# A two-layer block network on one core: the mLSTM recurrence with rows spread by transfers, a halved Fourier product, and the clamp of the exponent limited to the diagonal block

## The chip, the cores and the metric

The kernel runs on one core of a Trainium2 chip. The metric is the device time of one execution in microseconds (us); lower is better. Matrix products run on TensorE (PE; PEld is its weight load), elementwise work on VectorE (DVE), ScalarE (ACT) and GpSimd (POOL), and SyncE (SP) issues the transfers.

## The reference, cut to what matters

A sequence of 512 positions with 1024 channels goes through two layers of a first kind (feed-forward, a mixer of three branches, feed-forward, an embedding gate) and two of a second kind. All of the change lies in the mixer of the first kind, which runs twice. One projection makes the inputs of the three branches (attention, mLSTM, Fourier), 16 of its columns (m_if) are the gates of the mLSTM, and 64 (k_rope) the rotary key:

```python
u = rmsnorm(h, mix_norm[i]) @ w_in[i]
c_q, c_kv, k_rope, m_x, m_v, m_o, m_if, f_in = split_cols(u, IN_SPLITS)
```

The mLSTM, for 4 heads in 2 directions, weights scores by an exponential of gate sums; b is the running sum of log forget gates, and only s <= t counts:

```python
D = jnp.where(causal, b[..., :, None] - b[..., None, :] + ic[..., None, :], -jnp.inf)
m_t = jnp.maximum(m_inter, jnp.max(D, axis=-1))
w_intra = jnp.exp(D - m_t[..., None])
s = jnp.einsum('bhtd,bhsd->bhts', qc, kc) * w_intra
h = numer / jnp.maximum(jnp.abs(denom), jnp.exp(-m_t))[..., None]
```

The Fourier branch takes the real part of a two-dimensional transform over 512 positions and 64 channels of a group, and maps it linearly:

```python
y = jnp.fft.fftn(zg, axes=(1, 3), norm='ortho').real.astype(z.dtype)
return jnp.einsum('bsgc,gce->bsge', y, w).reshape(B, S, FNET_WIDTH) + b
```

## The kernel before, in words

Everything is held transposed, channels on the 128 partitions and the 512 positions along a row. Weights stream through one ring for the whole program: SP loads a tile of 128x1024 numbers (`Ring.load`, L400) into one of three raw buffers, ACT rounds it to a high part (L412), DVE makes the low part (L422), and PE multiplies high by high, high by low and low by high (L334 to L336), so one 128x1024 tile against 1024x512 inputs is 8x3 products. The ring is four tiles deep.

The program is a list of stages. Each is a block in which every engine runs its own list and which ends in a barrier (L243): the next stage starts when all engines, SP with its waits among them, have come to the end. Three stages matter here, each run once per layer.

**Projection** (`Project1`, last part of a longer stage). 11 column tiles, of which number 9 holds the rotary key twice over and number 10 the 16 gate columns, padded to 128 (`in1_g`); then four row parts of the ring for v and the Fourier input. PE: `Project.pe`; DVE copies each tile out of PSUM with the norm's factor; ACT adds the gates' biases (L1537, L1538), SP then loads the maps of the attention (L1503, L1504).

**Attention** (`mixer1_attention`). DVE computes the gate rows of the mLSTM at its start: 8 rows (4 heads, 2 directions) of 512 numbers each, on partitions 0 to 3 and 32 to 35, in `rows_a`, `rows_m`, `rows_t` (L1769 to L1774, semaphore `rows_ready`); the last come when ACT has taken an exponent (L1717).

**Recurrence** (`mixer1_mlstm`). No chunks: each head and direction is one masked product over all 512 positions. 8 groups g (head pair p, direction d, half e), each of 4 steps j, one per block of 128 source positions; a step spans 512, 384, 256 or 128 target positions (`span`). The 32 steps go through five engines, in an order written out by hand:

- PE spreads the row of the group over 128 partitions with a product into bank 2 or 3 (`spread`, L1887), once per group, and the bound rows into bank 7 once per pair of groups (L1920);
- DVE adds a column and clamps at 0, over the whole span (L2015), into one of four buffers `wgt`;
- ACT takes the exponent of the span (L1968);
- DVE multiplies by the scores (L2024), POOL masks the diagonal block (L2052);
- PE multiplies by v (L1937; the last group's steps L1934), and the buffer is free (`used`).

DVE's list for iteration s is: argument of step s, weighting of step s-1, then, in iterations 2 to 6 of the eight of a pair of groups from the second pair on, the bound of the pair before (L1994, L1996) and four reciprocals (L2000). Between its steps PE also makes the scores (`scores`, L1875, 16 of them; ACT copies them out, L1880) and the Fourier branch in bank 4 (`fourier`: L1854 four sums of four products, L1856 two sums of two, L1858 two products; ACT copies out, L1865, L1867). At the end DVE finishes the last pair in pieces (L2035 to L2043) while PE runs 8 products whose result nobody reads (`idle_products`, L358).

```python
dve.wait_ge(m_spread, g + 1)
dve.wait_ge(used, s_ - 3)
V.tensor_scalar(wgt[:, s_ % 4, r], ps[2 + g % 2][:, r], acol[:, j, rc:rc + 1], 0.0, ALU.add, ALU.min)
```

## Time and profile before

| | |
|---|---|
| median of 3 runs | 3802.32 us (3802.03 to 3806.3) |
| profiled execution | 3797.43 us |
| its span in the trace | 3795.7 us |
| PE busy | 97% of the span, 16570 products and as many weight loads |
| DVE, ACT, POOL busy | 58%, 34%, 20% |
| mean granted TensorE clock | 0.972 of full speed |

The profiled execution is 4.9 us below the median, and its span 1.7 us below its own time. A product of full 32-bit numbers stands in the trace as two records. A record's duration is from its start to its modelled end, and successive records overlap, so the pace of PE is read from the starts.

### The profile page before, as it was taken

The numbers are of one execution on the slowest core, as the hardware profiler recorded it, in microseconds if no ns is written. First come the engines' busy times: TensorE is split into PE (matmuls) and PEld (weight loads), VectorE is DVE, ScalarE is ACT, GpSimd is POOL, SyncE is SP. The second block draws the span as 40 slices with busy tenths as digits, with TensorE's granted clock in tenths as the row PEclk, the third lists the DMA queues.
The fourth block names the chain that finished last, engine by engine and source line by source line (L and its number), as shares of the span: only waits on it lengthen the run. The fifth ranks groups of instructions, "written<-read, shape, count | busy, mean of one in ns | idle before, by whom it ended". The sixth has DMA issues, their size and how long they took to land. (4 is left out here: it accounts for less than half of the span.)

```text
span 3795.7 us, 41460 instructions
## 1 busy us (share of the span) xinstructions
PE 3683.5 (97%) x16570; PEld 2860.5 (75%) x16570; DVE 2212.1 (58%) x2936; ACT 1297.3 (34%) x1876; POOL 744.9 (20%) x448
## 2 busy tenths in 40 slices
PE   8999999999999999999999999999999999999999
PEld 6888744888878888546888876786888767867887
DVE  7655557655575555457755576565544556645444
ACT  3223235422242223334422344444222343543221
POOL 3432002244204330001434013120000020300000
PEclk9999999999999999999999999898999998989999
DMA  5443200444334443102444322002333220012332
GB/s 175 144 137 116 94 24 23 135 137 131 125 100 134 136 134 102 60 24 89 140 132 138 102 79 61 6 1 67 95 95 100 83 79 21 1 51 85 99 100 83
DMA packets 93087, 345.40 MB, mean 91 GB/s; under 512 B 10977, under 2 KB 11233, under 8 KB 92001
## 3 DMA queue, kind: packets, MB, share of 16 engines
q1 hardware_dynamic: 92896, 342.76, 28.2%
q8 instruction: 132, 2.16, 0.2%
q14 instruction: 59, 0.48, 0.0%
HBM read 340.62 MB, written 2.10 MB: 90 GB/s over the span
## 5 line engine op out<-in xcount | busy, mean ns | idle before, releaser
L412 ACT ACTIVATE w_hi<-raw 128x1024 fp32r<-128x1024 f32 (+2 forms) x540 | 558.5, 1037 | 1814.1 <-PE ps L336 1733.1
L334 PE MATMUL ps<-xs_hi,w_hi 128*128 128x512 f32 x2312 | 911.3, 394 | 2.5 <-DVE arena L1300 2.5
L336 PE MATMUL ps<-xs_hi,w_lo 128*128 128x512 f32 x2312 | 903.6, 391 | 0.0
L335 PE MATMUL ps<-xs_lo,w_hi 128*128 128x512 f32 x2312 | 903.4, 391 | 0.0
L422 DVE TENSOR_TENSOR w_lo<-raw,w_hi 128x1024 fp32r<-128x1024 f32 (+2 forms) x540 | 676.0, 1253 | 148.0 <-ACT w_hi L412 147.4
L334 PEld LDWEIGHTS ps<-xs_hi,w_hi 128*128 128x128 f32 x2312 | 436.3, 189 | 105.0 <-issue 14.9
L335 PEld LDWEIGHTS ps<-xs_lo,w_hi 128*128 128x128 f32 x2312 | 436.2, 189 | 93.8 <-issue 3.6
L336 PEld LDWEIGHTS ps<-xs_hi,w_lo 128*128 128x128 f32 x2312 | 436.2, 189 | 91.5
L334 PE MATMUL ps<-hd_hi,w_hi 128*128 128x512 f32 x1288 | 503.3, 391 | 1.5 <-DVE hd_lo L1037 1.5
L336 PE MATMUL ps<-hd_hi,w_lo 128*128 128x512 f32 x1288 | 501.2, 389 | 0.0
L335 PE MATMUL ps<-hd_lo,w_hi 128*128 128x512 f32 x1288 | 501.1, 389 | 0.0
L827 POOL TENSOR_SCALAR arena<-arena,parg 128x768 f32<-128x768 f32 x128 | 305.4, 2397 | 955.7 <-DMA arena<-in_ada 697.6
L1033 DVE TENSOR_TENSOR arena<-arena,ps 128x512 f32<-128x512 f32 x132 | 90.7, 687 | 355.4 <-PE ps L336 350.7
L334 PEld LDWEIGHTS ps<-hd_hi,w_hi 128*128 128x128 f32 x1288 | 241.7, 188 | 53.1 <-DVE hd_lo L1037 2.0
L335 PEld LDWEIGHTS ps<-hd_lo,w_hi 128*128 128x128 f32 x1288 | 241.8, 188 | 51.0 <-issue 1.0
L336 PEld LDWEIGHTS ps<-hd_hi,w_lo 128*128 128x128 f32 x1288 | 241.7, 188 | 50.2
L835 POOL TENSOR_TENSOR arena<-arena 128x768 f32<-128x768 f32 x112 | 224.5, 2004 | 9.6 <-POOL arena L833 0.6
L1028 DVE TENSOR_TENSOR arena<-ps,stream_rstd 128x512 f32<-128x512 f32 x132 | 91.2, 691 | 230.9 <-PE ps L336 230.5
L1059 DVE SCALAR_TENSOR_TENSOR arena<-ps,stream_rstd 128x512 f32<-128x512 f32 x96 | 66.4, 691 | 156.9 <-PE ps L336 156.1
L2190 POOL TENSOR_SCALAR arena<-arena,par 128x512 f32<-128x512 f32 x4 | 10.3, 2582 | 671.7 <-DVE arena L2392 671.3
L1062 DVE TENSOR_TENSOR stream<-stream,arena 128x512 f32<-128x512 f32 x144 | 112.3, 780 | 4.9
L334 PE MATMUL ps<-ys_hi,w_hi 128*128 128x512 f32 x256 | 101.4, 396 | 2.7 <-DVE w_lo L422 2.7
(480 smaller groups left out, 4624.0 us busy)
## 6 DMA issues: line engine op xcount, KB each, us to landing
raw<-in_ffn_gu SPq DMA_DIRECT2D x264, 512.0 KB, 3.8
arena<-in_ada SPq DMA_DIRECT2D x64, 768.0 KB, 5.7
raw<-in_ffn_dn SPq DMA_DIRECT2D x96, 448.0 KB, 3.3
raw<-in_in_t SPq DMA_DIRECT2D x60, 512.0 KB, 3.7
raw<-in_ffn_dn SPq DMA_DIRECT2D x48, 512.0 KB, 3.5
raw<-in_out SPq DMA_DIRECT2D x32, 512.0 KB, 3.8
raw<-in_pleg SPq DMA_DIRECT2D x16, 512.0 KB, 3.7
raw<-in_in_r SPq DMA_DIRECT2D x8, 512.0 KB, 3.9
```

The costliest lines, as they stand in the source:

```text
L334: T.matmul(bank, lhs_hi(k), rhs_hi(k), start=(first and k == 0), stop=False)
L335: T.matmul(bank, lhs_hi(k), rhs_lo(k), start=False, stop=False)
L336: mm = T.matmul(bank, lhs_lo(k), rhs_hi(k), start=False, stop=(last and k == kt - 1))
L412: A.activation(self.hi[:, n % HL, 0:size], raw[:, n % RAW, 0:size], ACT.Copy).then_inc(self.high_done, 1)
L422: V.tensor_tensor(self.lo[:, n % HL, 0:size], raw[:, n % RAW, 0:size], self.hi[:, n % HL, 0:size].bitcast(F32), ALU.subtract).then_inc(sel ...
L827: G.tensor_scalar(aw[:, e, :], aw[:, e, :], cond(k0 + e), None, ALU.mult).then_inc(self.scaled, 1)
L835: ins = G.tensor_tensor(a, a, aw[:, e, :], ALU.add)
L1028: V.tensor_tensor(gn[:, j % 2, :], ps[2 * (j % 2)][:, :], R[:, :], ALU.mult).then_inc(self.gate_read, 1)
L1033: V.tensor_tensor(hf[:, j % 2, :], gn[:, j % 2, :], ps[2 * (j % 2) + 1][:, :], ALU.mult).then_inc(self.up_read, 1)
L1059: V.scalar_tensor_tensor(out=tmp[:, o % 2, :], in0=ps[4 + o % 2][:, :], scalar=self.scales[o], in1=R[:, :], op0=ALU.mult, op1=ALU.mult).th ...
L1062: V.tensor_tensor(h[:, o, :], h[:, o, :], tmp[:, o % 2, :], ALU.add).then_inc(self.h_updated, 1)
L2190: G.tensor_scalar(cv[:, c, :], cx[:, c, 0:S], w_(0), None, ALU.mult).then_inc(self.tap, 1)
```

## The change

- **Gates.** The 16 gate columns move into the tile of the rotary key (64 + 16 + 48 of zeros); `in1_g` is gone, and the projection has 10 column tiles and one item less in the ring. ACT makes the key's second copy. The gates come out on partitions 64 to 79; SP moves them with four small transfers to the partitions where the bias step reads them, after `spread` and behind the two map loads in its list, and ACT waits for them (`gates_moved`).
- **Rows by transfers.** The two `spread` kinds of product are gone. SP sends each of the eight rows of `rows_m` to all 128 partitions with a transfer (each 128 x 2 KB = 256 KB written, read from a row on one partition) during the attention: five after `rows_ready` has come to 3, three after `copied` has come to 14; SP waits for all of them before that stage's barrier. The bound rows `rows_t` go the same way in the recurrence stage, eight transfers of 128 KB, behind the loads of the Fourier table; DVE waits for all eight before its first bound.
- **Clamp.** DVE adds and clamps only the diagonal block of 128 positions, now from SBUF; ACT takes the rest of the span's exponent straight from the spread row with the column as bias, as a second instruction in 24 of 32 steps.
- **Fourier.** The table holds 257 cosines and 255 sines side by side (1 MB instead of 2 MB), so the first sum gives half of the frequencies of both kinds in one bank: 8 products instead of 16; the second step has 8 products of half width instead of 4; the copy mirrors the rest. They are spread over the 32 steps, one each 7/4 steps, in banks 4 and 7.

The core of the diff:

```diff
-            columns(t["in1_g"][l, :, :], 1)
...
-            super().__init__(st, x, source, 11, S)
+            super().__init__(st, x, source, 10, S)
...
+            sp.wait_ge(self.spread, 1)
+            for g in range(2):
+                for d in range(2):
+                    r = HD + 2 * H * g + H * d
+                    sp.dma_start(gate_rows[g][32 * d:32 * d + H, :], kr_tmp[r:r + H, :]).then_inc(self.gates_moved, 16)
             sp.wait_ge(self.next_landed, 32)
...
             act.wait_ge(self.spread, 1)
+            for half in (slice(0, HD), slice(HD, P)):
+                A.activation(kr[half, :], kr_tmp[0:HD, :], ACT.Copy)
+            act.wait_ge(self.gates_moved, 64)
...
+                sp.wait_ge(rows_ready, 3)
+                for g, dst in enumerate((soft, lf, F, a, M)):
+                    r = mlstm_row(g)
+                    sp.dma_start(dst, rows_m[r:r + 1, :].unsqueeze(1).to_broadcast([1, P, S])).then_inc(m_spread, 16)
+                sp.wait_ge(copied, 14)
+                for g in range(5, 8):
+                    r = mlstm_row(g)
+                    sp.dma_start(m_rows[:, g - 5, :], rows_m[r:r + 1, :].unsqueeze(1).to_broadcast([1, P, S])).then_inc(m_spread, 16)
+                sp.wait_ge(m_spread, 128)
...
+        FOURIER_AT = [7 * f // 4 for f in range(18)]
+        COPIED_AT = [FOURIER_AT[f] + 1 for f in (3, 7, 11, 15, 16, 17)]
...
-                sp.dma_start(dft.rearrange("p a j s -> p (a j s)"), t["dft"]).then_inc(dft_landed, 16)
+                sp.dma_start(dft.rearrange("p j s -> p (j s)"), t["dft"]).then_inc(dft_landed, 16)
                 sp.dma_start(fw.rearrange("p a m -> p (a m)"), t["fnw"][l, :, :]).then_inc(dft_landed, 16)
...
+                for q in range(4):
+                    for e in range(2):
+                        r = mlstm_row(2 * q + e)
+                        sp.dma_start(thr[HD * e:HD * e + HD, q, :], rows_t[r:r + 1, :].unsqueeze(1).to_broadcast([1, HD, S])).then_inc(t_spread, 16)
...
-                for g in range(2):
-                    spread(pe, g)
...
-                        if 1 <= g < 7:
-                            spread(pe, g + 1)
...
-                            T.matmul(ps[7][:, :], pick_pair(36, 5 * d + p), rows_t[0:36, :], start=True, stop=True).then_inc(t_spread, 1)
+                    if s_ in FOURIER_AT:
+                        fourier(pe, FOURIER_AT.index(s_))
...
-                    A.activation(wgt[:, s_ % 4, span(g, j)], wgt[:, s_ % 4, span(g, j)], ACT.Exp).then_inc(exp_ready, 1)
+                    own, rest = slice(j * P, (j + 1) * P), others(g, j)
+                    ins = A.activation(wgt[:, s_ % 4, own], wgt[:, s_ % 4, own], ACT.Exp)
+                    if rest.start < rest.stop:
+                        rc = mlstm_row(g)
+                        ins = A.activation(wgt[:, s_ % 4, rest], m_of[g][:, rest], ACT.Exp, bias=acol[:, j, rc:rc + 1])
+                    ins.then_inc(exp_ready, 1)
...
-                dve.wait_ge(thr_ready, q + 1)
-                order.done(V.scalar_tensor_tensor(out=larger, in0=dens[q % 2], scalar=-1.0, in1=thr[:, q % 2, :],
+                dve.wait_ge(t_spread, 128)
+                order.done(V.scalar_tensor_tensor(out=larger, in0=dens[q % 2], scalar=-1.0, in1=thr[:, q, :],
...
-                        r = span(g, j)
-                        if s_ % ST == 0:
-                            dve.wait_ge(m_spread, g + 1)
+                        r = slice(j * P, (j + 1) * P)
...
-                        V.tensor_scalar(wgt[:, s_ % 4, r], ps[2 + g % 2][:, r], acol[:, j, rc:rc + 1], 0.0, ALU.add, ALU.min) \
+                        V.tensor_scalar(wgt[:, s_ % 4, r], m_of[g][:, r], acol[:, j, rc:rc + 1], 0.0, ALU.add, ALU.min) \
```

`mlstm_row(g)` gives the partition of group g's row: 0, 1, 32, 33, 2, 3, 34, 35.

## Rows read from the trace of the kernel before

**Rows 1.** The page, part 1: busy time and share of PE.

```profile
PE 3683.5 (97%) x16570; PEld 2860.5 (75%) x16570; DVE 2212.1 (58%) x2936; ACT 1297.3 (34%) x1876; POOL 744.9 (20%) x448
```

**Rows 2.** Windows of layer one: stretch, length, five engines' busy time, granted clock, DMA.

```profile
427.00:445.00 18.00, 18.00 (x79) 14.53 (x78) 9.48 (x8) 4.97 (x6) 0.00 (x0) 1.00 0.30 88
...
568.00:574.00 6.00, 5.80 (x10) 2.16 (x8) 1.91 (x4) 3.10 (x6) 0.92 (x2) 0.50 0.18 71
...
590.00:595.00 5.00, 5.00 (x13) 1.96 (x12) 3.49 (x8) 3.10 (x7) 1.18 (x3) 1.00 0.00 0
...
625.00:630.00 5.00, 5.00 (x8) 1.96 (x8) 4.96 (x10) 1.52 (x3) 1.08 (x3) 0.56 0.00 0
```

**Rows 3.** Timeline of PE, end of the projection: start, duration, line, operation.

```profile
442.75 0.39 PE L334 MATMUL ps<-xs_hi,w_hi 128*128 128x512 f32 x1
...
443.20 0.39 PE L336 MATMUL ps<-xs_hi,w_lo 128*128 128x512 f32 x1
```

**Rows 4.** Timelines of ACT and PE after the column tiles.

```profile
449.47 0.72 ACT L1538 ACTIVATE arena<-arena,par 4x512 f32<-4x512 f32 x1
466.12 1.57 ACT L1470 ACTIVATE arena<-ps,rowsum 128x256 f32<-128x256 f32 x4 [15.93 <-PE ps L336]
```

**Rows 5.** Timeline of PE in the recurrence of layer one.

```profile
561.95 1.52 PE L1887 MATMUL ps<-arena,consts 36*128 36x512 f32 x3 [0.94 <-PEq L243]
...
581.82 1.02 PE L1854 MATMUL ps<-arena 128*128 128x512 f32 x2
582.68 1.02 PE L1937 MATMUL ps<-arena 128*128 128x512 f32 x2
...
589.59 0.49 PE L1937 MATMUL ps<-arena 128*128 128x128 f32 x2
...
633.43 3.70 PE L1934 MATMUL ps<-arena 128*128 128x128 f32 x20
```

**Rows 6.** Waits from 562 to 637 us: who waited, total, times, longest.

```profile
DVE arena L2024 <- ACT arena L1968: 20.4, 11, 5.3
...
PEld ps L1854 <- DMA arena<-in_fnw: 1.5, 1, 1.5
```

**Rows 7.** Groups of instructions from 562 to 645 us: busy, mean ns, idle before.

```profile
L2024 DVE TENSOR_TENSOR arena<-arena 128x512 f32<-128x512 f32 (+3 forms) x32 | 17.5, 547 | 20.4 <-ACT arena L1968 20.4
...
L2015 DVE TENSOR_SCALAR arena<-ps,arena 128x512 f32<-128x512 f32 (+3 forms) x32 | 16.4, 514 | 11.8 <-PE ps L1887 11.7
L1968 ACT ACTIVATE arena<-arena 128x512 f32<-128x512 f32 (+3 forms) x32 | 14.8, 466 | 10.5 <-DVE arena L2015 10.4
L2052 POOL TENSOR_TENSOR arena<-arena,consts 128x128 f32<-128x128 f32 x32 | 14.7, 462 | 107.9 <-DVE arena L2024 107.9
...
L2000 DVE RECIPROCAL arena<-arena 128x128 f32<-128x128 f32 x12 | 11.3, 945 | 0.0
...
L1994 DVE SCALAR_TENSOR_TENSOR arena<-arena 128x512 f32<-128x512 f32 x3 | 2.3, 760 | 2.3 <-ACT arena L1949 2.3
```

**Rows 8.** Groups by shape: clamps and exponents of 128 columns, a DVE scaling from SBUF.

```profile
L2015 DVE TENSOR_SCALAR arena<-ps,arena 128x128 f32<-128x128 f32 x8 | 2.5, 312 | 0.1
...
L1968 ACT ACTIVATE arena<-arena 128x128 f32<-128x128 f32 x8 | 2.5, 306 | 5.9 <-DVE arena L2015 5.9
...
L1790 DVE TENSOR_SCALAR arena<-arena 128x1 f32<-128x1 f32 x16 | 2.5, 154 | 0.5
```

**Rows 9.** DVE's last gate row, then SP's first issue of the recurrence stage.

```profile
495.41 0.42 DVE L1774 COPY arena<-arena 4x512 f32<-4x512 f32 x1
...
562.00 0.33 SPq L1840 DMA_DIRECT2D arena<-in_dft  x1
```

**Rows 10.** DMA: a load of 256 KB, two tables; positions (one row to 128 partitions).

```profile
arena<-in_dft SPq DMA_DIRECT2D x2, 2048.0 KB, 7.4
...
arena<-in_ukv SPq DMA_DIRECT2D x2, 1024.0 KB, 8.8
...
positions<-in_pos SPq DMA_DIRECT2D x2, 256.0 KB, 9.0
...
arena<-in_mqk SPq DMA_DIRECT2D x2, 256.0 KB, 3.3
```

**Rows 11.** DMA from 9 to 17 us, when all 16 engines are busy.

```profile
DMA packets 1573, 3.18 MB, mean 398 GB/s; under 512 B 544, under 2 KB 544, under 8 KB 1573
```

**Rows 12.** Timeline of DVE: a weighting beside POOL's 128x512 products.

```profile
620.32 1.82 DVE L2024 TENSOR_TENSOR arena<-arena 128x512 f32<-128x512 f32 x1
```

More of the change, by code:

```diff
@@ L1549, in dve @@
                     V.memset(mx[:, :, S + 2:S + 4], 0.0)
+                    for rows_ in gate_rows:
+                        V.memset(rows_[0:32, :], 0.0)
                     for i in range(2):
@@ L1553, in dve @@
                 dve.wait_ge(ring.used, self.n0 + j + 1)
[L1554 removed]
+                V.tensor_tensor(dst[j], ps[j % 4][:, :], R[:, :], ALU.mult).then_inc(self.spread if j == 9 else self.copied, 1)
                 if j:
@@ L1593, in program @@
     kr_tmp = arena[:, SPARE_AT:SPARE_AT + S]
+    gate_rows = [arena[:, SPARE_AT + (1 + g) * S:SPARE_AT + (2 + g) * S] for g in range(2)]
     def rotate(dve, order, x, turned, table, tmp):
@@ L1809, in mixer1_mlstm @@
         wgt = sp_.get(4, S)
-        thr, larger = conv, absf
+        larger = absf
+        m_of = [soft, lf, F, a, M] + [m_rows[:, i, :] for i in range(3)]
         dens, nums = [sp_.get(S), second[:, 0, :]], [sp_.get(S), second[:, 1, :]]
@@ L1827, in span, with others @@
             return slice(j * P, S) if groups[g][1] == 0 else slice(0, (j + 1) * P)
+        def others(g, j):
+            return slice((j + 1) * P, S) if groups[g][1] == 0 else slice(0, j * P)
         with Stage() as st:
@@ new lines, in fourier @@
+            def fourier(pe, f):
+                if f < 8:
+                    j, k = divmod(f, 4)
+                elif f < 16:
+                    j, k = 2 + (f - 8) // 4, f % 4
+                else:
+                    j, k = f - 12, 0
+                c = j % 2
+                bank = ps[4 if j % 2 else 7]
+                if f == 0:
+                    pe.wait_ge(dft_landed, 32)
+                if j >= 2 and k == 0:
+                    pe.wait_ge(dft_copied, j - 1)
+                if j < 2:
+                    mm = T.matmul(bank[:, :], vz[:, k, 384 + c * P:384 + (c + 1) * P], dft[:, k, :], start=(k == 0), stop=(k == 3))
+                elif j < 4:
+                    src = part[:, c, MID + 1:S] if k % 2 else part[:, c, 1:MID] if k else part[:, c, 0:MID + 1]
+                    dst = bank[:, MID + 1:S] if k >= 2 else bank[:, 1:MID] if k else bank[:, 0:MID + 1]
+                    lhs = C("dft_c") if k % 2 == 0 else C("dft_n") if k == 3 else C("dft_s")
+                    mm = T.matmul(dst, lhs, src, start=(k % 2 == 0), stop=(k % 2 == 1))
+                else:
+                    mm = T.matmul(bank[:, :], fw[:, c, :], spec[:, c, :], start=True, stop=True)
+                if f in (3, 7, 11, 15, 16, 17):
@@ L1863, in fourier_copy @@
                 act.wait_ge(dft_done, j + 1)
-                if j < 6:
-                    ins = A.activation(part[:, j // 2, j % 2, :] if j < 4 else spec[:, j - 4, :], ps[4][:, :], ACT.Copy)
+                bank, c = ps[4 if j % 2 else 7], j % 2
+                if j < 2:
+                    ins = A.activation(part[:, c, :], bank[:, :], ACT.Copy)
+                elif j < 4:
+                    A.activation(spec[:, c, 0:MID + 1], bank[:, 0:MID + 1], ACT.Copy)
+                    ins = A.activation(spec[:, c, MID + 1:S], bank[:, S - 1:MID:-1], ACT.Copy)
                 else:
-                    ins = A.activation(y[:, j, :], ps[4][:, :], ACT.Identity, bias=col(l, c1, "fnet_b", j - 6))
+                    ins = A.activation(y[:, 6 + c, :], bank[:, :], ACT.Identity, bias=col(l, c1, "fnet_b", c))
                 ins.then_inc(dft_copied, 1)
@@ L1880, in scores_copy @@
                 A.activation(qks[:, m // 8, m % 2, m // 2 % ST, :], ps[m % 2][:, :], ACT.Copy).then_inc(qk_copied, 1)
-            def spread(pe, g):
-                p, d, e = groups[g]
-                if g >= 2:
-                    pe.wait_ge(arg_ready, ST * (g - 1))
-                T.matmul(ps[2 + g % 2][:, :], pick(36, 32 * d + 2 * p + e), rows_m[0:36, :], start=True, stop=True) \
-                 .then_inc(m_spread, 1)
             @st.block.tensor
             def _(pe):
-                for g in range(2):
-                    spread(pe, g)
                 for m in range(4):
@@ L1973, in _ @@
                         scores_copy(act, 6 + 2 * g + k)
-                    if k == 0 and e == 1:
-                        act.wait_ge(t_spread, q + 1)
-                        if q >= 2:
-                            act.wait_ge(dir_ready, q - 1)
-                        A.activation(thr[:, q % 2, :], ps[7][:, :], ACT.Copy).then_inc(thr_ready, 1)
                     if k == 1 and e == 0 and q:
@@ L3315, in lay_out @@
     cq, ckv, kr, mx, mv, mo, mif, fin = [w[:, :, o[i]:o[i + 1]] for i in range(8)]
-    f["in1_t"] = tile_pairs(np.concatenate([cq, ckv, mx, mo, kr, kr], 2))
-    gates = np.zeros((L, D, P), np.float32)
-    for g in range(2):
-        for d in range(2):
-            r = 64 * g + 32 * d
-            gates[:, :, r:r + H] = mif[:, :, 8 * g + 4 * d:8 * g + 4 * d + 4]
-    f["in1_g"] = rows(gates)
+    rest = np.zeros((L, D, 48), np.float32)
+    f["in1_t"] = tile_pairs(np.concatenate([cq, ckv, mx, mo, kr, mif, rest], 2))
     f["in1_r"] = rows(np.concatenate([mv, fin], 2))
```

91 lines of the change are left out of this document (34 added, 57 removed).

## The prediction

> **What bounds the kernel now.** The page comes first: PE is busy for 97% of the span, every other engine for 58% or less [rows 1]. So time comes off where PE has less to do, as long as PE is what the others wait for there. The windows say where that holds. In the projection PE is busy throughout at full clock and DVE half the time (427 to 445 us) [rows 2]. In the recurrence (562 to 637 us in layer one; layer two has the same shape) PE is busy too, but its clock is at the lower of its two levels (0.50, 1.2 GHz) after the barrier, back at the upper one by the middle, and low again from about 625 us [rows 2]. The waits and groups give the rest: POOL idles 107.9 us of DVE's weightings, DVE idles 11.7 us on the spread products and 20.4 us on ACT's exponents [rows 6, 7], which are late because ACT's list holds score copies that wait for PE. This stage is bound by PE first, and the DVE-ACT-DVE-POOL-PE round of a step stands right behind.
>
> **Part 1, the projection.** Starts of products lie (443.20 - 442.75)/2 = 0.225 us apart [rows 3]. One tile less is 24 products, 5.4 us per layer, and nothing covers it: the load, rounding and subtraction of a tile are all shorter than that. The detour of the gates is costed at nothing. Today the bias steps end at 450.2 us and ACT then has nothing until PE's row parts end at 466.1 [rows 4]. The four small transfers stand behind SP's two map loads, 8.8 us to landing for the later [rows 10]; ACT's two key copies and four bias steps (0.72 us each) follow. With everything 5.4 us earlier, the maps are issued near 443.5, the gates land near 454, the bias steps end near 457, and ACT is wanted at 460.7. Some 3.5 us of cover is left; beyond that, each us late is one lost at the next barrier.
>
> **Part 2, PE in the recurrence.** A full product of 512 columns takes 582.68 - 581.82 = 0.86 us at the upper clock [rows 5]. Gone are 8 spreads, 4 bound spreads, and of the Fourier branch's 22 products the worth of 8 (8 + 8 halves + 2 = 14): 20 x 0.86 = 17.2 us per layer. The last product now ends at 633.43 + 3.70 = 637.1 [rows 5], 75 us after SP's first issue of the stage [rows 9].
>
> I take the stage in its four pairs of groups. The first ends at 590.1, 28.1 us in [rows 5]. Off it go two spreads at low clock ahead of everything (1.9 us, from the 1.52 us for three of their four records), the wait for the Fourier tables (1.5 us [rows 6], the big one half as large) and, later, two spreads or bound spreads and three Fourier products (8 become 5), 5 x 0.86 = 4.3 us. That leaves 20.4 us.
>
> **Part 3, DVE, the next bound.** For each of the other pairs DVE has 8 weightings at 0.55, 8 clamps, a bound of two instructions at 0.76 and four reciprocals at 0.945 [rows 7]. A clamp of 128 columns from SBUF is not in the trace: 0.154 us (one column) and 0.312 us (128 columns from PSUM) are its ends [rows 8]; I take 0.2, since the fixed part dominates. Sum 4.4 + 1.6 + 1.5 + 3.8 = 11.3 us. Overlap of neighbours takes about 1 off, and meeting POOL puts something on. That meeting is in the trace: a weighting of 512 columns took 1.82 us beside POOL's large products [rows 12] against a mean of 0.55. I take 12.3 us a pair, between 10.3 (no meeting) and 15 (each of POOL's 0.46 us masks stops DVE once: 8 x 0.46 = 3.7 more). PE needs 4.3 us of products a pair, plus 1.7 to 5.5 of scores and Fourier, and fits.
>
> The Trainium skill has a rule that speaks against this part: "SBUF — State Buffer", section "Who interferes with whom", lets a single-source DVE instruction between SBUF operands take both ports and stop GpSimd for its whole length, which a clamp that reads PSUM does not. By it each clamp holds up a mask by its own 0.2 us or waits one out; the end of 15 us would be nearer. The weightings already show such stops; for clamps no row does.
>
> ACT's 24 extra instructions cost a fixed 0.2 us each (a 128-column exponent takes 0.306 [rows 8], for some 0.1 of columns), 1.2 us a pair; four threshold copies leave. ACT is busy for half the stage, so this is costed at nothing, and its price in a step's round, 0.2 us, is within the 12.3.
>
> Sum: 20.4 + 3 x 12.3 = 57.3, and 2.7 for the way through POOL and PE at the end and a low clock there: 60 us against 75, 15 per layer. The tail of DVE and the barrier stay as they are.
>
> **Part 4, the transfers.** This is the unknown. Eight of 256 KB may start when the last gate row stands, at 495.8 us, and the barrier falls just before 562.0 [rows 9]: 66 us of cover, which moves with everything else, so they are hidden up to 8 us each. The eight of 128 KB stand behind the Fourier table (3.7 us, half of 7.4 [rows 10]), while DVE's first bound comes about 23.5 us into the stage (20.4 and two steps): hidden if 0.8 + 3.7 + 4T < 23.5, where T is the time of 256 KB, so up to T = 4.7. The trace has no transfer out of SBUF of this kind. The low end is 256 KB in 3.3 us from issue to landing, alone [rows 10], of which the moving takes only 0.66 us at 398 GB/s [rows 11]. The high end by kind is the only broadcast of one row to 128 partitions, 9.0 us [rows 10], but that one stood in the crowd of the first loads, as the 398 GB/s around it show, and may have waited most of it. If one row's readers share a sixteenth of that rate, 25 GB/s, T is 10.5. I take the side of 3.3, being nearest in size and undisturbed: hidden.
>
> **The sum.** 2 x (5.4 + 15) = 41 us off. Against the profiled 3797.4 that is 3756.4; the median stands 4.9 us higher, so 3761 us.
>
> **Rivals.**
>
> A, slower: the source row is the limit. All eight rows lie on one partition each, and 16 engines read the same one. Place: SP's wait ahead of the attention's barrier, and DVE's wait at the first bound. Price per layer: the barrier comes 8T + 2 - 66 us later; the first bound comes at 4T + 4.5, and 1.5 for the bound and 22 steps at 1.54 (12.3/8) follow, so the last product ends at 4T + 40 against 75. With 5.4 gained, the net is 12T - 104.4: it turns at T = 8.7. At T = 9.6, between 9.0 and 10.5, the net is 10.8 us a layer, 3824 us in all. For it: the 9.0 us row, and that one partition cannot be expected to feed what 128 do. Against it: nothing in this trace is seen to be limited by its source. The Trainium skill gives a rule for it in "SBUF — State Buffer", section "Door 1: The DMA port swizzle": the rate depends on how many of 16 ports the partitions reach, partitions 0 to 3 and 32 to 35 share a single port, and four partitions were measured at 27.6 GB/s. By that rule T would be 9.5 us and the kernel slower; no run here shows it yet. Chance 0.34.
>
> B, half hidden: T between 4.7 and 8. The attention covers its eight, the bounds come late; at T = 6 the last product ends at 64, 11 us a layer from that stage, 3769 us. Chance 0.10.
>
> C, the meeting of DVE and POOL or the low clock: 15 us a pair. PE, with gaps between its bursts, may fall to its lower level, as it did after the gap before 625 us [rows 2], and then needs twice 6 to 10 us a pair. The stage loses 8 us of its gain, 3777 us. Chance 0.06.
>
> D, the change does not do what it says for the recurrence: the round of a step, not PE's amount, sets the pace, and the stage stays at 75 us. Only the projection is left, 3791 us. Against it stand windows with PE busy for all 5 of 5 us at full clock and DVE for 3.5 (590 to 595 us) [rows 2]. Chance 0.06.
>
> **How the numbers follow.** The forecast's own case has 0.44 and a range of its own, 3747 (10.3 us a pair: 12 us less in two layers) to 3772. A reaches from 3805 (T near 8.8) to beyond 3840. From 3747 to 3828, some 2 in 10 is left out: the upper part of A and the lowest of the forecast. 0.2% is 7.6 us, about what a measurement of this kernel can tell from no change. Faster by more: 0.43 of the forecast, 0.09 of B, 0.05 of C, 0.03 of D, 0.60. Slower by more: 0.29 of A. The rest, 0.11, is within.
>
> **What would show it.** Right: the projection's last tile ends 5.4 us earlier; the eight transfers of 256 KB land before the attention's last product, and SP is not the last at the barrier; DVE never waits for `t_spread`; the last product comes about 60 us into the stage, and DVE's idle time there is small. Wrong: the barrier waits for a transfer (PE idle for 10 us or more between attention and recurrence, as in A); one long idle time of DVE at the first bound, 23 us in (A, B); weightings or clamps well above their lengths beside POOL, or clock 0.50 in the middle of the stage (C); ACT waiting for `gates_moved` until after PE's row parts (part 1).

## The result, and the profile after

The changed kernel takes 3828.09 us (3827.43 to 3830.23, four runs) beside 3802.18 us of the kernel before on the same chip: 1.0074 of its time, with a 95% interval of 1.0059 to 1.0089. It is slower by 0.7%. That is rival A; the forecast's own case (3761) did not come, and the median lies 0.09 us above the range's upper end of 3828.

The table splits the executions of both kernels, and of two experiments told below, by stage. Projection is from SP's first load of `in_in_t` to its issue of `in_mqk`, attention from there to its issue of `in_dft`, recurrence from there to the first product of the ring behind it. Each pair is layer one and layer two, in us.

| | projection | attention | recurrence | six stages | span |
|---|---|---|---|---|---|
| before | 118.9, 119.0 | 93.8, 93.7 | 86.4, 85.3 | 597.0 | 3795.7 |
| after | 115.8, 114.3 | 106.8, 105.0 | 90.2, 90.4 | 622.5 | 3825.7 |
| e4, no transfers of rows | 115.8, 114.3 | 90.4, 93.7 | 71.0, 73.1 | 558.2 | 3759.7 |
| e5, rows by way of DRAM | 115.8, 114.3 | 90.4, 93.7 | 70.9, 73.1 | 558.1 | 3758.1 |

The six stages explain 25.5 of the 30.0 us between the spans; the rest is 2.2 us at the program's start and 2.3 elsewhere, and in other runs of this study those parts move by as much with nothing changed in them.

The page after: PE's busy time and products fell against [rows 1], while its share fell to 95% because it waits; the DMA queue's share rose from 28.2% to 32.8%, although the kernel reads fewer bytes from DRAM (337.5 MB instead of 340.6; the table is half as large).

```profile
PE 3635.4 (95%) x16458; PEld 2837.7 (74%) x16458; DVE 2202.1 (58%) x2936; ACT 1299.3 (34%) x1918; POOL 741.0 (19%) x448
...
q1 hardware_dynamic: 96256, 346.04, 32.8%
```

SP's timeline of layer one (start, length of the issues, line, transfer):

```profile
447.86 0.43 SPq L1503 DMA_DIRECT2D arena<-in_uq  x1
448.34 0.43 SPq L1504 DMA_DIRECT2D arena<-in_ukv  x1
448.81 2.68 SPq L1509 DMA_DIRECT2D arena<-arena  x4
467.34 0.34 SPq L1662 DMA_DIRECT2D arena<-in_mqk  x1
494.97 27.19 SPq L1666 DMA_DIRECT2D arena<-arena  x5
522.21 28.87 SPq L1670 DMA_DIRECT2D arena<-arena  x3
574.13 0.34 SPq L1875 DMA_DIRECT2D arena<-in_dft  x1
574.53 0.42 SPq L1876 DMA_DIRECT2D arena<-in_fnw  x1
574.99 28.25 SPq L1880 DMA_DIRECT2D arena<-arena  x8
```

Five issues that should take some 2 us take 27: the queue takes no more until earlier transfers have moved on. The eight start at 494.97. SP's last issue ends at 551.08 and SP then waits 22.6 us for the transfers, so the last has landed at 573.7 and one takes (573.7 - 494.97) / 8 = 9.8 us; the barrier lets PE go at 574.09. The groups of transfers after (size, median from issue to landing, with the time in the queue):

```profile
arena<-arena SPq DMA_DIRECT2D x16, 256.0 KB, 32.4
arena<-in_dft SPq DMA_DIRECT2D x2, 1024.0 KB, 4.8
arena<-arena SPq DMA_DIRECT2D x16, 128.0 KB, 17.5
```

PE's timeline shows the price at the barrier: its 16 idle products end at 560.1 and the next work comes at 574.09, 14.0 us idle, where it was 0.94 in the kernel before [rows 5]. Later it waits 16.7 us, because DVE waited for the bound rows:

```profile
553.10 7.03 PE L326 MATMUL ps<-arena 128*128 128x512 f32 x16
574.09 2.08 PE L1926 MATMUL ps<-arena 64*128 64x512 f32 x4 [13.96 <-PEq L243]
...
617.86 1.22 PE L1964 MATMUL ps<-arena 128*128 128x256 f32 x2 [16.71 <-POOL arena L2076]
...
650.83 1.83 PE L1961 MATMUL ps<-arena 128*128 128x128 f32 x14 [0.73 <-POOL arena L2076]
```

DVE's timeline at the first and second bound, and its wait over both layers (sum, times, longest):

```profile
615.25 0.69 DVE L2021 SCALAR_TENSOR_TENSOR arena<-arena 128x512 f32<-128x512 f32 x1 [16.40 <-DMA arena<-arena]
...
629.93 0.69 DVE L2021 SCALAR_TENSOR_TENSOR arena<-arena 128x512 f32<-128x512 f32 x1 [1.15 <-ACT arena L1976]
```

```profile
DVE arena L2021 <- DMA arena<-arena: 32.2, 2, 16.4
```

The windows (columns: PE, PEld, DVE, ACT, POOL busy, granted clock, DMA share, GB/s) show what the queue does meanwhile: 90% busy, and no more than 27 to 28 GB/s, against 398 GB/s in [rows 11]. They also show the clock at its lower level in the stage's first 5 us, after PE had stood idle.

```profile
520.00:530.00 10.00, 10.00 (x34) 5.07 (x33) 6.07 (x16) 2.34 (x6) 0.00 (x0) 1.00 0.90 27
560.00:570.00 10.00, 0.13 (x1) 0.00 (x0) 0.00 (x0) 0.60 (x1) 0.00 (x0) 0.66 0.90 28
574.00:579.00 5.00, 4.26 (x8) 1.52 (x8) 0.48 (x2) 1.16 (x3) 0.00 (x0) 0.50 0.82 252
...
610.00:615.00 5.00, 0.00 (x0) 0.00 (x0) 0.00 (x0) 0.00 (x0) 0.00 (x0) 0.50 0.68 23
```

### The profile page after: what moved, and what is told of

Read it like the earlier page. It is cut to its first block and busy times, and to the rows that moved or that the text cites. A ratio compares the mean times of both kernels' runs of the same rounds, so it can differ in the third digit from the quotient of the medians.

```text
span 3825.7 us, 41288 instructions
## 1 busy us (share of the span) xinstructions
PE 3635.4 (95%) x16458; PEld 2837.7 (74%) x16458; DVE 2202.1 (58%) x2936; ACT 1299.3 (34%) x1918; POOL 741.0 (19%) x448
## 3 DMA queue, kind: packets, MB, share of 16 engines
q1 hardware_dynamic: 96256, 346.04, 32.8%
## 5 line engine op out<-in xcount | busy, mean ns | idle before, releaser
L412 ACT ACTIVATE w_hi<-raw 128x1024 fp32r<-128x1024 f32 (+2 forms) x538 | 556.1, 1037 | 1811.5 <-PE ps L336 1731.6
L2214 POOL TENSOR_SCALAR arena<-arena,par 128x512 f32<-128x512 f32 x4 | 10.3, 2584 | 668.8 <-DVE arena L2416 668.4
```

Source lines behind the costliest of these rows:

```text
L412: A.activation(self.hi[:, n % HL, 0:size], raw[:, n % RAW, 0:size], ACT.Copy).then_inc(self.high_done, 1)
L2214: G.tensor_scalar(cv[:, c, :], cx[:, c, 0:S], w_(0), None, ALU.mult).then_inc(self.tap, 1)
```

## The experiments

All start from the changed kernel. e1 to e4 leave out the rows or put constants in their place, so their results are not those of the network. e1, e2, e3, e7, e8 and e9 were run once, the others four times and e10 six times. Differences of a few us are read from the six stages rather than from medians, since the rest of the program moves by 3 us or more between executions.

### Is the source the limit? (e1)

```diff
-sp.dma_start(dst, rows_m[r:r + 1, :].unsqueeze(1).to_broadcast([1, P, S]))
+sp.dma_start(dst, conv[:, 0, :])
```

(and alike for `m_rows`; `thr` reads `conv[HD * e:HD * e + HD, 1, :]`, and POOL fills `conv` with constants first)

> As the changed kernel, but each of the 16 transfers per layer reads as many bytes from a tile on 128 (or 64) partitions in place of one row on one partition; the destinations, the bytes written and the places in SP's list are the same (the recurrence so computes on filled-in rows: two constants that POOL writes). Theory S, the one partition read by all engines is the limit: 256 KB lands in 3 to 5 us, the barrier of the attention no longer waits, DVE's wait at the first bound (16.4 us in the changed kernel) is gone, total near 3771 us. Rival R1, the number of issues and descriptors of SP is the limit, and rival R2, any transfer out of SBUF is slow: nothing changes, 9 to 10 us for each 256 KB and a total near 3828 us.

3761.83 us, one run. The same number of transfers of the same sizes, from 128 partitions instead of one, and both waits are gone:

```profile
492.86 3.14 SPq L1667 DMA_DIRECT2D arena<-arena  x5
496.88 1.76 SPq L1671 DMA_DIRECT2D arena<-arena  x3
557.38 0.34 SPq L1881 DMA_DIRECT2D arena<-in_dft  x1
```

```profile
arena<-arena SPq DMA_DIRECT2D x16, 256.0 KB, 2.5
```

So it is neither the number of SP's issues nor the destinations nor the attention's own traffic. What is left is the source, one row on one partition.

### The two places, one at a time, and both (e2, e3, e4)

e2 drops the eight transfers of m rows (POOL fills the buffers with a constant), e3 those of the bound rows, e4 both.

```diff
-                for g, dst in enumerate((soft, lf, F, a, M)):
...
-                sp.wait_ge(m_spread, 128)
+                sp.wait_ge(m_spread, 8)
...
+                for dst in (soft, lf, F, a, M, m_rows[:, 0, :], m_rows[:, 1, :], m_rows[:, 2, :]):
+                    G.memset(dst, -200.0).then_inc(m_spread, 1)
```

> Leaves out the eight transfers of 256 KB per layer; POOL sets their destinations to a constant in the attention stage. The eight of 128 KB stay. Theory S: the attention's stage is as long as before the change (93.7 us instead of 107), the stall at the first bound stays at 16 us; 2 x 12 us less than the changed kernel, near 3804 us. Rival W, the longer attention stage is not SP's wait but contention with the attention's own work: DVE, ACT or PE instructions of that stage get shorter too.

3804.47 us. Attention 92.1 and 90.3 us, recurrence 92.1 and 92.4, with a wait at the first bound that is 3.6 us longer than after, since DVE comes to it earlier:

```profile
DVE arena L2018 <- DMA arena<-arena: 39.7, 2, 20.0
```

> Leaves out the eight transfers of 128 KB per layer; POOL sets the bound rows to 1. The eight of 256 KB stay. Theory S: no wait at the first bound, 2 x 16.4 us less than the changed kernel, near 3795 us; the attention's stage stays near 107 us. Rival G, the recurrence is held by its own round of steps: less than half of that comes back.

3795.86 us. The attention keeps its 105.1 and 105.0 us; the recurrence takes 73.8 and 74.1.

> Leaves out all 16 transfers per layer, with constants in their place: what the rest of the change is worth with the transfers free. My prediction's own case: 3761 us, the last product of the recurrence 60 us into its stage. By the changed kernel's trace, less its two waits: 3828 - 2 x (12 + 16.4) = 3771 us. Rival G: above 3785.

3759.67 us (3751.49 to 3761.94, four runs), 0.9887 of before with 0.9868 to 0.9906. The two places add up nearly: against the six stages of after (622.5), e2 has 25.7 us less, e3 34.5 and e4, without both, 64.3. Part of the 4 us between shows in the clock: e3 still has the wait at the barrier, its recurrences start with a granted clock of 0.50 over the first 5 us, and the first bound comes 26.1 and 26.4 us in, against 22.2 and 25.1 in e4. The forecast of 3761, whose case was "all transfers hidden", is met to 1.3 us by the kernel that has none. That it is met so closely is in part luck: over both layers the projection gave 7.8 us of 10.8 forecast and the recurrence 27.6 of 30, and the attention, for which nothing was forecast, 3.4.

### Partition, port or queue? (e8, e9)

e8 lets ACT's queue issue four of the eight, beside SP's four, each from other partitions (0, 1, 32, 33 and 2, 3, 34, 35):

```diff
+                act.wait_ge(rows_ready, 3)
+                act.wait_ge(copied, 14)
+                for g in range(4, 8):
+                    r = mlstm_row(g)
+                    act.dma_start(m_of(g), rows_m[r:r + 1, :].unsqueeze(1).to_broadcast([1, P, S])).then_inc(m_spread, 16)
```

> Four of the eight 256 KB transfers are issued from ACT's queue, the other four from SP's, at the same time; each queue reads its own partitions (0, 1, 32, 33 on one, 2, 3, 34, 35 on the other), all of one port by the skill's table. ACT is held up by its own issues, so the total says little. Theory P (the single partition is the limit, each partition apart): the two queues run side by side, all eight land within 40 to 45 us of the first issue (78 with one queue). Rival Q (the port shared by these eight partitions is the limit): the two share it, all eight need 75 us or more. Rival R (the rings of one queue are the limit): as P.

Two queues moved together what one did, 27 to 28 GB/s; the last landed between 565 and 570 us, 78 us after the first issue at 491.5. The windows of e8:

```profile
510.00:520.00 10.00, 0.00 (x0) 0.00 (x0) 0.00 (x0) 0.00 (x0) 0.00 (x0) 0.50 0.92 28
...
550.00:560.00 10.00, 10.00 (x33) 4.99 (x33) 6.10 (x17) 2.84 (x8) 0.00 (x0) 1.00 0.92 28
```

e9 is the same, but ACT's four read copies that DVE makes on other partitions:

```diff
+                V.tensor_copy(rows_m[64:68, :], rows_m[0:4, :])
+                V.tensor_copy(rows_m[96:100, :], rows_m[32:36, :]).then_inc(rows_ready, 1)
...
-                    r = mlstm_row(g)
+                    r = mlstm_row(g) + 64
```

> As e8, but ACT's four transfers read copies of their rows on partitions 66, 67, 98 and 99 (two more copies by DVE), a port other than that of partitions 0 to 3 and 32 to 35 by the skill's table. e8 moved 26 to 29 GB/s with both queues at work, so the single partition is not the limit. Theory Q (a shared port of the source is): about 54 GB/s while both queues have work, all eight land some 40 to 45 us after the first issue instead of 78. Rival V (anything that reads single rows out of SBUF in 16 engines runs at 27 GB/s in all, wherever the row is): 27 GB/s again, 78 us.

From 500 to 510 us, just after ACT's first issue at 499.2, the rate was 27 and then 38 GB/s; over the next 25 us it was 43 to 59 in each stretch of 5 us, and it fell back to 27 when only ACT's were left:

```profile
510.00:515.00 5.00, 0.00 (x0) 0.00 (x0) 0.00 (x0) 0.00 (x0) 0.00 (x0) 0.50 0.94 54
...
530.00:535.00 5.00, 5.00 (x10) 1.96 (x8) 2.15 (x6) 1.24 (x3) 0.00 (x0) 0.76 0.93 59
...
540.00:545.00 5.00, 5.00 (x20) 2.64 (x19) 4.64 (x13) 1.61 (x5) 0.00 (x0) 1.00 0.85 27
```

All eight had landed by 550, 55 us after the first issue at 495.1 (40 to 45 expected; the queues overlapped only in part, ACT began 4 us later and ended last). So the limit is neither the single partition (e8) nor single rows as such (e9), but something that neighbouring partitions share (in e8 both queues read 0 to 3 first and 32 to 35 after them) and that 66, 67, 98 and 99 do not share with 0, 1, 32 and 33. Whether 0 to 3 share it with 32 to 35 as well is not shown apart: only around the changeover can e8 have read both sets at once, and the rate stayed at 27 to 28 there. The Trainium skill calls it a port: "SBUF — State Buffer", section "Door 1: The DMA port swizzle", puts 0 to 3 and 32 to 35 on port 0 and 66, 67, 98 and 99 on port 1, and gives four partitions 27.6 GB/s. The measured 27 to 28 agree. That both whole times (3866.07 and 3851.96 us, one run each) are worse than after lies mostly in the attention, 123.3 and 114.1 us in layer one instead of 106.8: ACT is held at its issues for 37 and 26 us, and PE and DVE stand idle meanwhile.

### The rows by way of DRAM (e5)

```diff
+                for i, rows_ in enumerate((rows_m, rows_t)):
+                    for d in range(2):
+                        sp.dma_start(t["spread"][l, 8 * i + 4 * d:8 * i + 4 * d + 4, :], rows_[32 * d:32 * d + 4, :]).then_inc(stored, 16)
+                sp.wait_ge(stored, 64)
...
-                    sp.dma_start(dst, rows_m[r:r + 1, :].unsqueeze(1).to_broadcast([1, P, S])).then_inc(m_spread, 16)
+                    sp.dma_start(dst, kept(0, l, g).partition_broadcast(P)).then_inc(m_spread, 16)
```

(`kept` is the row in the scratch; the other two sets of transfers change alike)

> The sixteen rows are stored once to a scratch in DRAM (four transfers of 8 KB) and all sixteen broadcasts read them from there; nothing else changes. Theory S (a single SBUF partition as the source is what limits a transfer to 9.8 us per 256 KB): the loads from DRAM take 3 to 5 us each, two stores add some 3 us well ahead of need, no wait at the attention's barrier and none at the first bound, 3763 us (3755 to 3772). Rival R3 (one row read by all is the limit wherever it is kept; the broadcast of `positions` from DRAM took 9.3 us): T stays near 9 us, the wait at the barrier stays at 16 us or more, 3820 to 3835 us.

3760.13 us (3759.91 to 3769.01, four runs), 0.9898 of before with 0.9883 to 0.9913: faster than both kernels, and the stages of e4, which has no transfers. The timeline and the transfers of e5:

```profile
494.93 1.30 SPq L1672 DMA_DIRECT2D spread_rows<-arena  x4
497.37 2.24 SPq L1675 DMA_DIRECT2D arena<-spread_rows  x5
499.65 1.38 SPq L1678 DMA_DIRECT2D arena<-spread_rows  x3
```

```profile
arena<-spread_rows SPq DMA_DIRECT2D x16, 256.0 KB, 5.0
arena<-spread_rows SPq DMA_DIRECT2D x16, 128.0 KB, 5.0
positions<-in_pos SPq DMA_DIRECT2D x2, 256.0 KB, 10.3
```

Storing and reading back costs 2.4 us ahead of the first load; the eight loads then pass at over 300 GB/s (322 in the window from 500 to 505 us). The row of `positions`, a broadcast from DRAM as well, stands at 10.3. Since 256 KB broadcast from DRAM can land in 5.0, its kind of source is not what makes it slow; the crowd of first loads around it is the likely reason.

### The wait of the first bound alone (e7)

```diff
-                dve.wait_ge(t_spread, 128)
+                dve.wait_ge(t_landed[q], 32)
```

> The wait for all eight bound rows at the first bound becomes a wait for the two rows of its own pair; transfers unchanged. Theory (the first bound only waits because its semaphore counts all eight; the rows come one pair each 10 us from 5 us into the stage, each pair of groups takes 12 us or more): no wait for a transfer in the recurrence, stage 74 instead of 90 us, 3796 us (3788 to 3803); the attention keeps its 105 us. Rival (the queue of slow transfers delays every pair in turn, the wait is only spread out): DVE still waits 10 us or more in sum, 3815 us or more.

3790.89 us, with no wait of DVE for a transfer in the recurrence and 73.9 and 74.0 us for the stage. Sixteen of the 90 us came from one semaphore counting all eight rows where two are needed. In its one run the kernel with this edit alone lies below every one of the seven runs of before beside it (3796.6 to 3804.84). Another run of before, on another chip, took 3787.58, so a gain over before is likely and not shown.

### Where the recurrence's gain comes from (e6, e11, e12, e13, e14)

e6 makes the m rows by products again (full clamps from PSUM, one exponent) and keeps the bound rows as transfers, moved into the attention:

```diff
-                    own, rest = slice(j * P, (j + 1) * P), others(g, j)
...
+                    A.activation(wgt[:, s_ % 4, span(g, j)], wgt[:, s_ % 4, span(g, j)], ACT.Exp).then_inc(exp_ready, 1)
...
+                for g in range(2):
+                    spread(pe, g)
```

> Only the m rows go back to PE products (8 per layer at 0.86 us, read by DVE from PSUM, clamping the whole span, one exponent per step); the bound rows stay transfers, moved to the attention, where some 41 us of them fit into 66 us. Theory S with the prices of my parts 2 and 3: no wait for a transfer; PE has 6.9 us more per layer than in the kernel without transfers (3759.7 us), DVE's 32 clamps take 0.51 instead of 0.2 us, 10 us per layer, of which the part beside POOL's waits is partly hidden: 3774 us (3765 to 3790). Rival D (the round of a step sets the pace in the recurrence, products do not matter): stage as before, 3790 us or more. If the small clamps are what made the stage short rather than PE's load, it is 3785 or more too; below 3768 says PE's load was it.

3775.86 us (0.9939 of before, 0.9923 to 0.9956); recurrence 76.2 and 76.7.

e11 is e5 with the small clamps and the split exponent undone, the rows still in SBUF:

```diff
-                        r = slice(j * P, (j + 1) * P)
+                        r = span(g, j)
```

> e5's kernel with DVE clamping each step's whole span again, from the spread rows in SBUF, and one exponent per step; PE's load and the transfers as in e5. It tells what the small clamps bring by themselves. My part 3 (DVE bounds the later pairs; a clamp of 512 columns from SBUF costs 0.1 to 0.3 us more than one of 128): 3 to 9 us a layer more, 3766 to 3778 us. Rival (the round of a step does not rest on DVE, or the shorter chain through ACT pays for it): 3760 us.

3758.4 us (0.9886, 0.9865 to 0.9908), six stages 558.4 against e5's 558.1: with the rows in SBUF, the small clamp by itself brings nothing that the totals can tell. DVE's groups show what it saves there. In layer one of e11 the four lengths of clamp sum to 13.6 us:

```profile
L2042 DVE TENSOR_SCALAR arena<-arena 128x256 f32<-128x256 f32 x8 | 4.5, 561 | 0.0
...
L2042 DVE TENSOR_SCALAR arena<-arena 128x512 f32<-128x512 f32 x8 | 3.7, 456 | 7.2 <-PEq L243 7.1
...
L2042 DVE TENSOR_SCALAR arena<-arena 128x384 f32<-128x384 f32 x8 | 3.4, 421 | 0.0
...
L2042 DVE TENSOR_SCALAR arena<-arena 128x128 f32<-128x128 f32 x8 | 2.0, 251 | 0.1
```

In layer one of e5 the 32 small ones take 10.4:

```profile
L2047 DVE TENSOR_SCALAR arena<-arena 128x128 f32<-128x128 f32 x32 | 10.4, 328 | 8.4 <-PEq L243 7.1 <-PE ps L1971 1.2
```

The 3.2 us less of DVE's time do not reach the stage's end: recurrence 144.0 us in e5, 144.3 in e11 (how far this pair can be trusted is said below the table). That ACT's second instruction takes them back is likely, and not shown.

e12, e13 and e14 put work back into e5: twelve products that nobody reads at the places of the spreads; the bound rows' products with ACT's four copies; eight products beside the first eight of the Fourier branch.

```diff
+                    if k == 1 or k == 3 and e == 0:
+                        idle_products(ps[2][:, :], 1)
```

> e5's kernel with PE given the twelve products of 512 columns per layer back that the spreads were (into an unused bank, at the places where they stood: one a group and one more in every second group), read by nobody. Parts 2 and 3 of my sum: only the first pair is bound by PE, so three of them count there, at 0.86 us or twice that at the low clock: 2.6 to 5 us a layer, 3765 to 3770 us. Rival (PE bounds all four pairs): 12 x 0.86 = 10.3 us a layer, 3780 us. Rival (busy PE keeps its upper clock, and gains from it): 3760 us or less.

```diff
+                            T.matmul(ps[3][:, :], pick_pair(36, 5 * d + p), rows_t[0:36, :], start=True, stop=True).then_inc(t_spread, 1)
...
+                        act.wait_ge(t_spread, q + 1)
+                        A.activation(thr[:, q, :], ps[3][:, :], ACT.Copy).then_inc(thr_ready, 1)
```

> e5's kernel with the bound rows spread by PE again (four products per layer, into a free bank, ACT's four copies, where they stood before); the m rows come from DRAM as in e5. Four products are 3.4 us of PE's time per layer and four copies 2.4 us of ACT's. Theory E (in the recurrence the hand-over between engines sets the pace: ACT's list, which waits for PE's product before it can take the next exponent, costs more than the product itself): 2 to 5 us a layer, 3764 to 3770 us. Theory P (only PE's amount counts, at the 1.7 to 4 us a layer that twelve products cost in e12): 0.6 to 1.4 us a layer, 3761 to 3763 us.

```diff
+                if f < 8:
+                    idle_products(ps[2][:, :], 1)
```

> e5's kernel with each of the first eight Fourier products doubled by a product of 512 columns that nobody reads, so that PE has the eight products per layer back that the halved table saves. Theory P (as in e12): 8/12 of what e12 cost, 1.2 to 3 us a layer, 3762 to 3766 us. Theory F (in the first pair PE is what all wait for, as in part 2 of my sum; five of the eight stand there, 0.86 us each): 4.3 us a layer, 3769 us. Rival: nothing, 3760 us, then the halved table's gain lies in its order and its banks, not in its amount.

| | median, us | recurrence, both layers | against e5, per layer |
|---|---|---|---|
| e5 | 3760.13 | 144.0 | |
| e11, full clamps | 3758.4 | 144.3 | 0.1 |
| e13, bound rows by product | 3767.12 | 146.5 | 1.3 |
| e12, twelve idle products | 3768.83 | 147.4 | 1.7 |
| e14, eight products at the Fourier's places | 3770.59 | 150.3 | 3.1 |
| e6, m rows by product | 3775.86 | 152.9 | 4.4 |
| before | | 171.7 | 13.8 |

The recurrences are read from one trace of each kernel. e1, e4 and e10, whose recurrence does the same work as e5's, stand at 144.3, 144.1 and 145.0. The single layers of these four take 70.9 to 72.0 us where the granted clock was at 1.00 in the stage's first 5 us, and 73.0 or 73.1 where it was near 0.7, as in layer two of e5. So 0.5 us a layer cannot be told from nothing. In e6, e11 and e13 both layers began at 1.00, so the table puts them too low by part of a us a layer: e11's 72.3 and 72.0 stand 0 to 1.4 us above the layers with small clamps and the same clock, and a worth of the clamp of about 1 us a layer is not excluded.

The medians stand further above e5's than the recurrences do (by 5.3 us more in e12, 4.5 in e13, 4.2 in e14, 6.8 in e6). Part of it is seen in the attentions, which take 90.3 to 95.4 us in these traces with no edit in them; the rest was not located, and the shares below are the stage's own.

The eight products at the Fourier's places cost nearly twice what the twelve at the spreads' places do: five of the eight stand in the first pair of groups, and three of the twelve. There PE's work delays the others: the first bound comes 23.4 and 25.0 us into the stage in e5, 24.1 and 26.5 in e12, and 25.9 and 28.0 in e14, which is 2.5 and 3.0 of e14's 3.7 and 2.6 us more in the stage. The m rows' products cost more than products alone, because DVE's first clamp waits for the first of them. In layer one its idle time before the clamps, which begins ahead of the barrier, is 10.5 us in e6 and ended by the spread, where e5 has 7.1 ended by the barrier:

```profile
L2042 DVE TENSOR_SCALAR arena<-ps,arena 128x512 f32<-128x512 f32 x8 | 5.7, 712 | 10.5 <-PE ps L1932 10.5
```

The shares of e6, e13 and e14 together are 8.8 of the 13.8 us per layer, if they may be added, which no run with all three shows. The other 5 (the Fourier branch's order, its second bank, its smaller second step, the clock at the stage's start) were not taken apart.

### The projection's missing microseconds (e10)

```diff
-                    for rows_ in gate_rows:
-                        V.memset(rows_[0:32, :], 0.0)
...
+                if j == 2:
+                    for rows_ in gate_rows:
+                        V.memset(rows_[0:32, :], 0.0)
```

> e5's kernel (rows through DRAM), and the two memsets of the gate rows stand behind the third copy instead of ahead of the first. Theory: they delay the first copy by 0.7 us, the row products behind it fall late and PE's clock drops for some us after; without them 1 to 2.3 us a layer come back, 3756 us (3754 to 3759). Rival (the low clock near 400 us comes from elsewhere): 3760 as e5.

After, the sums of squares of PE wait 1.03 us for DVE instead of 0.31 in the kernel before, and in layer one the clock dips for some us behind them:

```profile
400.69 1.05 PE L1432 MATMUL ps<-consts,stream_squares 128*128 128x1 f32 x8 [1.03 <-DVE arena L1564]
```

```profile
399.00:407.00 8.00, 6.97 (x28) 5.37 (x28) 5.07 (x6) 1.32 (x2) 0.00 (x0) 0.79 0.35 109
```

In layer two the wait is the same 1.03 us, and the clock does not dip:

```profile
1510.60:1518.60 8.00, 6.97 (x35) 5.56 (x34) 5.11 (x6) 1.32 (x2) 0.00 (x0) 1.00 0.33 108
```

In e10, where the stage starts 2.0 us earlier, the wait is back at 0.30 us and there is no dip:

```profile
397.00:405.00 8.00, 7.70 (x38) 6.18 (x37) 5.66 (x9) 1.63 (x3) 0.00 (x0) 1.00 0.38 125
```

The projections take 113.5 and 113.5 us, 2.3 and 0.7 less than in e5: 0.7 for the wait in each layer, and 1.6 for the dip where there was one. The dip does not follow the wait each time: of the 28 projections of the fourteen kernels with the memsets ahead, 15 have it and take 115.7 to 115.9 us, and 13 do not and take 114.1 to 114.3; of the four of before and e10 none has it. The six stages fall by 2.0 us to 556.1, while the median, 3762.51 us (3757.26 to 3765.76, six runs, 0.9902 with 0.9886 to 0.9919), cannot be told from e5's. The 0.7 us of the wait are shown in the stage; that the longer wait makes the dip possible fits all the traces, what decides between dip and none is open, and a gain in the whole time is not shown.

## Why the prediction was wrong, and where it was right

**Part 4 is the step that failed**, in its last sentence: "I take the side of 3.3, being nearest in size and undisturbed: hidden." A transfer of 256 KB from one row takes 9.8 us, three times that, and it lies between the two ends (9.0 and 10.5) that the part had for a limited source. The row of 3.3 us was near in bytes written and far in what matters, since its bytes came from a whole tensor. The part even named the size that decides, 25 GB/s as a sixteenth of 398; measured are 27 to 28. A rule by which the choice could have been made is to ask which resource the new transfer has less of than every row in the trace, and here that was the source.

**Rival A** was right in its mechanism, its two places and its sizes. With T = 9.8 its formulas give, and the trace shows: the barrier 14.4 us later, 13.0 and 11.3 in the table; the first bound 43.7 us into the stage, 41.1 (615.25 - 574.13); the last product ends at 79.2, 78.5; net 13.2 us a layer, 12.7. Only its point, T = 9.6, was a little low, and so the range ended just short. The weak argument was "nothing in this trace is seen to be limited by its source": a trace without one single-row source in SBUF cannot show it, so the sentence was no evidence, and the chance of 0.34 leaned on it.

**Part 1**: 5.4 us a layer forecast, 3.1 and 4.7 measured. The 24 products are gone as forecast; the 0.7 us of PE's longer wait for DVE are missing in both layers and 1.6 us of low clock in layer one. The detour of the gates is hidden as costed: ACT idles 10.3 us for the transfers, its bias steps start at 457.95, and it still waits 4.4 us for PE's row parts (3.5 forecast).

```profile
ACT arena L1545 <- DMA arena<-arena: 10.3, 1, 10.3
ACT arena L1469 <- PE ps L336: 4.4, 1, 4.4
```

That part's step "everything 5.4 us earlier, the maps are issued near 443.5" did not hold (447.86, after 448.75 in the kernel before), and did not matter. What it left out were the two new memsets of DVE ahead of the first copy, and the clock that can fall behind them (e10).

**Parts 2 and 3**, with the rows hidden (e4, e5): first bound forecast 23.5 us into the stage, 23.4 measured in layer one of e5 and 25.0 in layer two; pairs 12.3, and 13.2 and 12.5, in layer two 13.3 and 13.0; last product at 60, and 59.2 and 61.4. DVE's bounds in layer one of e5:

```profile
582.74 0.69 DVE L2028 SCALAR_TENSOR_TENSOR arena<-arena 128x512 f32<-128x512 f32 x1 [1.15 <-ACT arena L1983]
...
595.97 0.69 DVE L2028 SCALAR_TENSOR_TENSOR arena<-arena 128x512 f32<-128x512 f32 x1 [1.15 <-ACT arena L1983]
...
608.46 0.68 DVE L2028 SCALAR_TENSOR_TENSOR arena<-arena 128x512 f32<-128x512 f32 x1
```

The stages fell by 15.5 and 12.2 us against 15 forecast. (The own case's lower end of 3747 is a slip of its working, which takes 12 us off 3761 and so gives 3749; nothing rests on it.) The term of the small clamp was mis-sized, 0.33 us in the mean for 0.2, and what it stands for is worth at most about 1 us a layer (e11): the account of DVE's time was near, and as a reason for the gain it was wrong, since the 3.2 us more of clamps in e11 did not come back in the stage. The meeting with POOL that part 3 feared is there, not at the masks but beside POOL's products of 512 columns (a clamp after took 0.19 to 0.29 us beside the masks and 1.29 us at 626.40). By the Trainium skill's rule on it, "SBUF — State Buffer", section "Who interferes with whom", the prediction put the pair near 15 us as an estimate; the traces of e5 have 12.5 to 13.3.

**Rivals B, C and D.** B had T below 8, and it is 9.8. C's pairs of 15 us did not come, but its mechanism is there in small: after, the clock is low with the waits (0.50 behind the barrier and at 610 us), and in e5, where nothing waits for a transfer of rows, it also falls between the second and third bound, behind a stretch in which PE had gaps:

```profile
594.38:599.38 5.00, 2.95 (x9) 1.74 (x10) 3.78 (x9) 2.77 (x8) 1.00 (x3) 1.00 0.01 2
599.38:604.38 5.00, 3.79 (x9) 1.96 (x8) 4.81 (x11) 4.18 (x12) 1.84 (x5) 0.73 0.00 0
```

These two bounds are still only 12.5 us apart. D is refuted by e5's stages of 71 and 73 us, and by e14, where PE's amount counts.

## What to carry to other kernels

- A broadcast whose source is a row on one partition is priced by its source, by the bytes written over what that source yields. Here that was 9.8 us per 256 KB, and a second queue on neighbouring partitions did not help, where the same row from DRAM takes a place in a stream of over 300 GB/s. Store it once and read it back, if 2.4 us ahead of need can be had.
- When a price is bounded by two rows, choose by the resource in which the new transfer differs from both, not by size.
- A semaphore that counts all of a set where the reader needs the first two cost 16 us a layer here; and undoing the clamp by itself showed that this part of the change brought at most about 1 us a layer.
- A short low clock can come or stay away with the same instructions, so one stage of one trace is compared with all stages that do the same work before a difference of 1 or 2 us is given a cause.

## What was not expected of the hardware

- An issue is not free when the queue is full. SP's five issues took 27.2 us, ACT's four 36.9 us (e8); on ACT that stopped the attention.
- Two queues do not add up when both read rows on partitions 0 to 3 and then 32 to 35 (27 to 28 GB/s for both together), and mostly do when one reads 66, 67, 98 and 99 (43 to 59 GB/s).
- Two memsets of 32x512 on DVE cost 0.7 us a layer of PE idle time, and in 15 of 28 cases a granted clock of 0.79 over 8 us and 1.6 us more; in the other 13 the clock stayed at 1.00.
- In layer one of e11 a clamp of 256 columns took longer on average (0.56 us) than one of 512 (0.46); in layer two both took 0.44. Two of the former took 1.35 us each (at 592.91 and 606.82), beside POOL's products of 512 columns (1.71 us from 592.40 and 606.31); the others took 0.25 to 0.35.
